# mLSTM heads kept in PSUM through square, root and gating, with the causal addition of the second tile placed first

## The chip, the core and the metric

The kernel runs on one core of a Trainium2 chip. It is written for the five engines of the core directly: TensorE (PE) multiplies, VectorE (DVE), ScalarE (ACT) and GpSimd (POOL) work element by element, and SyncE (SP) issues the loads. Each has its own queue that runs in the order written, and they wait for one another by semaphores. The metric is the device time of one execution in microseconds, the median of several runs.

## The reference

256 tokens of width 1024 pass through a stack of blocks: feed-forward layers, one mLSTM mixer, one differential attention, a second model part with convolution and attention. The change lies in the mLSTM mixer alone. With four heads, keys of 128 and values of 256 columns, in two chunks of 128 tokens, what matters is:

```
d   = where(causal, b[t] - b[s] + li[s], -inf)          # b: running sum of the log forget gates
m_t = max(b[t] + m, max over s of d)
w   = exp(d - m_t);  s_inter = exp(b + m - m_t)
qk  = (q k^T) * w
num = qk v + s_inter * (q C)
den = sum(qk) + s_inter * (q n)
h   = num / max(|den|, exp(-m_t))
h   = h * rsqrt(mean(h*h over the head) + EPS) * head_norm
return (sigmoid(o) * h) @ w_out
```

## The kernel before, in words

All large products are made in three parts, so that they keep fp32 accuracy: a rounded weight `w_hi`, the rest `w_lo`, and the same two parts of the activations (`xT_hi`, `xT_lo`). Weights come in slots of 2048 columns. For every slot SP loads `w_raw`, ACT rounds it to `w_hi` (L548, 1.9 us, called through `ahead`, four slots in advance), POOL subtracts to get `w_lo` (L519, four operations of 128x512), and PE runs twelve matmuls of 512 columns per slot and tile of 128 tokens (L1614 to L1622). The order of all other work is written out by hand for each engine.

The mLSTM stage has twelve slots of the input product ("MI", six chunks of 512 columns: q, k, two of v, two of the output gate o) and four of the output product ("MO"). PE fits the small mLSTM products between the tiles of chunks 2 to 5 (`chunk(c, amid)`):

- `spread(t)` brings the per-token gate terms of tile t into PSUM (`tb[:, 0]`); DVE's `causal_max(t)` adds the causal mask (L1183) and takes the maximum of each head (L1186). ACT turns the masked terms into exponentials (L715, L723).
- `turn_qk(0)` and `turn_qk(1)` (L1848) transpose q and k into `tb` after the first and the second tile of chunk 4; ACT copies them out (L732). Before the first of them PE waits for `m_am_ready` 2, which DVE gives when the negated maximum of tile 1 is written (L1206).
- The scores (L1855), the state (L1878) and its use (L1894), the transposed weights (L1861) and the two numerators (L1867) follow. Tile 0's numerators go to `gu`, tile 1's to `acc[:, :, 0:512]`.
- DVE multiplies the numerators with 1/denominator into `m_h` in SBUF (L1250; for tile 1 L1256 adds the parts and L1258 multiplies). ACT squares `m_h` and sums each head (L754). DVE takes the root in eleven steps on four columns (`rsqrt_steps`, L996 to L1005), each of which waits for the one before (`link`). The output gate is a sigmoid from PSUM into `m_sig` (L743, `output_gate(c, t)`), multiplied with the gain (L1265, `gate_gain(c, t)`). Last come four products per tile (L1279).
- `t_of_h(t)` lets PE transpose the result (L1667) after the third tile of chunk 5 (t = 0) and inside the output product (t = 1). It waits for `m_y_ready`.

`acc`, `gu` and `tb` are PSUM; `arena` in the rows is the large SBUF buffer that holds all `m_...` tiles. `pair(c, t)` is the PSUM half in which chunk c of tile t is accumulated: `acc[:, t, 0:512]` for c = 4, `acc[:, t, 512:1024]` for c = 5.

## Time and profile before

| what | value |
|---|---|
| median of 3 runs | 1434.67 us (1431.86 to 1436.09) |
| the profiled execution: its own time | 1433.08 us |
| its span, first to last instruction | 1431.2 us |
| PE busy | 1378.9 us (96%) |
| POOL busy | 1135.1 us (79%) |
| ACT busy | 658.3 us (46%) |
| DVE busy | 462.4 us (32%) |
| mean granted clock of PE | 0.990 |

The profile is of one execution. Busy times count each engine by itself, and they overlap. Idle time of DVE or ACT says nothing as long as PE does not wait for them. A granted clock of 1.00 is 2.4 GHz on PE, 0.50 is 1.2 GHz. The mLSTM stage lies at about 216 to 315 us of the span.

### The profile page before, as it was taken

What the parts mean: (1) busy time and instruction counts of PE and PEld (TensorE: products, weight loads), DVE (VectorE), ACT (ScalarE), POOL (GpSimd) and SP (SyncE); (2) the same over time, 40 slices, a digit from 0 to 9 for tenths busy, and PEclk for the clock granted to TensorE, in tenths of its full rate; (3) what the DMA queues carried; (4) which work ended last, traced back from release to release, by engine and by line L of the source; (5) the groups of instructions that cost most, each with busy time, mean ns of one, the idle gap of its engine ahead of it and who ended that gap; (6) DMA issues with size and microseconds to landing.
All of it is one profiled execution on the core that took longest, in us unless ns stands there. A gap on an engine that the chain in (4) does not pass through costs nothing.

```text
span 1431.2 us, 18160 instructions
## 1 busy us (share of the span) xinstructions
PE 1378.9 (96%) x6396; PEld 1127.5 (79%) x6396; DVE 462.4 (32%) x1108; ACT 658.3 (46%) x763; POOL 1135.1 (79%) x912
## 2 busy tenths in 40 slices
PE   7999999989999999999999789999999999999996
PEld 5888878877888877888888567888877877788785
DVE  6011044464000165210013665100156134552234
ACT  5444345536434365453435565443446443544431
POOL 5999977649999968899997509989877976679873
PEclk9999999999999999999999899999999999999999
DMA  8666544526665545656565406656554544346541
GB/s 258 209 205 206 192 160 174 165 74 218 191 194 178 199 151 193 192 192 195 176 196 185 136 1 191 206 186 194 177 174 165 194 160 147 120 146 234 185 141 42
DMA packets 160669, 246.95 MB, mean 173 GB/s; under 512 B 8892, under 2 KB 99812, under 8 KB 160484
## 3 DMA queue, kind: packets, MB, share of 16 engines
q1 hardware_dynamic: 158324, 239.42, 51.4%
q10 hardware_dynamic: 2288, 6.75, 1.3%
q8 instruction: 37, 0.61, 0.2%
q14 instruction: 20, 0.16, 0.0%
HBM read 245.10 MB, written 1.05 MB: 172 GB/s over the span
## 4 chain that ended last, share of the span: by engine, by line
POOL 46%; PE 35%; issue 15%; DVE 2%; ACT 1%; DMA 0%; POOLq 0%; ACTq 0%; DVEq 0%
POOL w_lo L519 46%; PE acc L1614 5%; PE acc L1617 5%; PE acc L1615 5%; PE gu L1614 3%; PE gu L1615 3%; PE gu L1617 3%; PE acc L1647 1%; PE acc L1653 1%; PE acc L1650 1%; PE gu L2004 1%; PE tb L1614 1%; PE tb L1617 1%; PE tb L1615 1%; PE tb L2013 1%
## 5 line engine op out<-in xcount | busy, mean ns | idle before, releaser
L519 POOL TENSOR_TENSOR w_lo<-w_raw,w_hi 128x512 fp32r<-128x512 f32 x896 | 1130.0, 1301 | 272.2 <-ACT w_hi L548 272.2
L548 ACT CAST w_hi<-w_raw 128x2048 fp32r<-128x2048 f32 x225 | 424.8, 1907 | 117.6 <-DMA w_raw<-in_w_ffn_in 34.1
L1614 PE MATMUL gu<-w_hi,xT_hi 128*128 128x512 f32 x832 | 331.4, 398 | 5.0 <-DVE w_lo L1545 2.8
L1615 PE MATMUL gu<-w_lo,xT_hi 128*128 128x512 f32 x832 | 325.7, 391 | 0.0
L1617 PE MATMUL gu<-w_hi,xT_lo 128*128 128x512 f32 x708 | 276.8, 391 | 0.0
L1614 PE MATMUL acc<-w_hi,xT_hi 128*128 128x512 f32 x544 | 218.7, 402 | 3.5 <-DVE xT_lo L1033 2.6
L1615 PE MATMUL acc<-w_lo,xT_hi 128*128 128x512 f32 x544 | 212.8, 391 | 0.0
L1617 PE MATMUL acc<-w_hi,xT_lo 128*128 128x512 f32 x512 | 200.8, 392 | 0.0
L1614 PEld LDWEIGHTS gu<-w_hi,xT_hi 128*128 128x128 f32 x832 | 157.3, 189 | 37.3 <-DVE xT_lo L1033 3.2
L1615 PEld LDWEIGHTS gu<-w_lo,xT_hi 128*128 128x128 f32 x832 | 157.5, 189 | 31.2 <-issue 0.2
L1092 DVE SCALAR_TENSOR_TENSOR arena<-gu,rstd,arena 128x256 f32<-128x256 f32 x88 | 42.3, 484 | 371.2 <-ACT arena L622 371.0
L1617 PEld LDWEIGHTS gu<-w_hi,xT_lo 128*128 128x128 f32 x708 | 133.4, 188 | 28.3
L622 ACT ACTIVATE arena<-gu,rstd 128x256 f32<-128x256 f32 x88 | 41.3, 474 | 201.0 <-PE gu L1617 196.1
L1614 PEld LDWEIGHTS acc<-w_hi,xT_hi 128*128 128x128 f32 x544 | 102.9, 189 | 24.6 <-issue 3.7
L1615 PEld LDWEIGHTS acc<-w_lo,xT_hi 128*128 128x128 f32 x544 | 103.0, 189 | 19.9 <-issue 0.2
L1617 PEld LDWEIGHTS acc<-w_hi,xT_lo 128*128 128x128 f32 x512 | 96.6, 189 | 20.8
L1647 PE MATMUL acc<-w_hi,hT_hi 128*128 128x512 f32 x336 | 103.9, 391 | 0.0
L1653 PE MATMUL acc<-w_hi,hT_lo 128*128 128x512 f32 x336 | 103.7, 390 | 0.0
L1650 PE MATMUL acc<-w_lo,hT_hi 128*128 128x512 f32 x336 | 103.6, 390 | 0.0
L1099 DVE TENSOR_TENSOR hT_lo<-tb,hT_hi 128x512 fp32r<-128x512 f32 x40 | 27.7, 692 | 208.1 <-ACT hT_hi L638 208.1
L638 ACT CAST hT_hi<-tb 128x512 fp32r<-128x512 f32 x40 | 23.4, 585 | 123.4 <-PE tb L1702 123.4
L1653 PEld LDWEIGHTS acc<-w_hi,hT_lo 128*128 128x128 f32 x336 | 63.1, 188 | 13.1
(300 smaller groups left out, 1289.3 us busy)
## 6 DMA issues: line engine op xcount, KB each, us to landing
w_raw<-in_w_ffn_in SPq DMA_DIRECT2D x176, 512.0 KB, 4.7
w_raw<-in_w_ffn_out SPq DMA_DIRECT2D x88, 512.0 KB, 4.2
w_raw<-in_w_in SPq DMA_DIRECT2D x80, 512.0 KB, 4.5
w_raw<-in_mlstm_w_in SPq DMA_DIRECT2D x24, 512.0 KB, 4.6
w_raw<-in_w_ple_gate SPq DMA_DIRECT2D x16, 512.0 KB, 4.3
w_raw<-in_w_kv SPq DMA_DIRECT2D x16, 512.0 KB, 4.5
w_raw<-in_mlstm_w_out SPq DMA_DIRECT2D x8, 512.0 KB, 4.5
w_raw<-in_diff_w_q SPq DMA_DIRECT2D x8, 512.0 KB, 4.1
```

What stands on the lines that cost most here:

```text
L519: ins = pool.tensor_tensor(w_lo[:, slot.spl, cols], w_raw[:, slot.raw, cols], w_hi[:, slot.spl, cols].bitcast(F32), ALU.subtract)
L548: nc.scalar.copy(w_hi[:, slot.spl, :], w_raw[:, slot.raw, :]).then_inc(hi_ready, 1)
L622: nc.scalar.activation(sg[:, t, :], gu[:, t, 0:CH], ACT.Silu, scale=rstd[:, 2 * m + t:2 * m + t + 1]).then_inc(silu_ready, 1)
L638: nc.scalar.copy(hT_hi[:], tb[:, 0, :].rearrange("p (k c) -> p k c", k=2)).then_inc(ht_hi_ready, 1)
L1092: v.scalar_tensor_tensor(hs[:, t, :], gu[:, t, CH:2 * CH], rstd[:, 2 * m + t:2 * m + t + 1], sg[:, t, :], ALU.mult, ALU.mult).then_inc(h_r ...
L1099: v.tensor_tensor(hT_lo[:], tb[:, 0, :].rearrange("p (k c) -> p k c", k=2), hT_hi[:].bitcast(F32), ALU.subtract).then_inc(ht_lo_ready, 1)
L1614: mm(out, xh, wh, start=(half == 0 and k == 0), stop=False)
L1615: mm(out, xh, wl, start=False, stop=False)
L1617: last = mm(out, xl, wh, start=False, stop=(half == 1 and k == 3))
L1647: mm(acc[:, t, 512 * half:512 * half + 512], a_hi[:, k, tok(t)], w(w_hi, half), start=st, stop=False)
L1650: mm(acc[:, t, 512 * half:512 * half + 512], a_hi[:, k, tok(t)], w(w_lo, half), start=False, stop=False)
L1653: last = mm(acc[:, t, 512 * half:512 * half + 512], a_lo[:, k, tok(t)], w(w_hi, half), start=False, stop=sp_)
```

## The change

Three edits, all in the mLSTM stage.

1. On DVE, `causal_max(1)` moves ahead of the small differences for tile 0's exponents, and its addition releases the new semaphore `m_spread_used`. PE waits for that before `turn_qk`, no longer for the finished maximum. On ACT, the rounding `ahead(s0 + 8)` and the copies of the turned q move ahead of the small exponentials.
2. The heads stay in PSUM. The product with 1/denominator is gone as an operation: ACT squares the numerators with 1/denominator as its scale, and DVE multiplies the finished root with 1/denominator (four columns). The last products read the numerators from `gu`. Tile 1's parts are added into `gu` after tile 0's products. The intermediate values of the root (`mean`, `tmp`, the last step) lie in `tb[:, 1]`.
3. The output gate's sigmoid is written in place in PSUM, and `gate_gain` reads it there; PE's second numerators wait for `m_gain_ready`. The gate of chunk 5, tile 0 moves ahead of the rounding `ahead(s0 + 11)`.

The diff, cut to its core:

```diff
@@ ScalarE, mlstm
                 ins.then_inc(m_w_ready, 1)
+                ahead(At(s0 + 8))
+                def turned_qk(i):
+                    for w in (2 * i, 2 * i + 1):
+                        act.wait_ge(m_pl_in_psum, w + 1)
...
+                turned_qk(0)
                 act.wait_ge(m_exps, 1)
                 nc.scalar.activation(m_exp0, m_exp0, ACT.Exp).then_inc(m_exped, 1)
-                ahead(At(s0 + 8))
                 act.wait_ge(m_am_ready, 2)
...
-                for w in range(4):
...
-                    if w == 1:
-                        ahead(At(s0 + 9))
+                ahead(At(s0 + 9))
+                turned_qk(1)
                 ahead(At(s0 + 10))
...
-                    nc.scalar.activation(m_sig[:, t, 512 * (c - 4):512 * (c - 4) + 512], pair(c, t),
-                                         ACT.Sigmoid, scale=rstd[:, 2 * m + t:2 * m + t + 1]
-                                         ).then_inc(m_o_gate, 1)
+                    nc.scalar.activation(pair(c, t), pair(c, t), ACT.Sigmoid,
+                                         scale=rstd[:, 2 * m + t:2 * m + t + 1]).then_inc(m_o_gate, 1)
...
-                    act.wait_ge(m_h_ready, t + 1)
+                    if t == 0:
+                        act.wait_ge(m_num_in_psum, 1)
+                        act.wait_ge(m_rden_ready, 1)
+                    else:
+                        act.wait_ge(m_h_ready, 1)
                     for h in range(MH):
                         ins = nc.scalar.activation(squares[:, MDV * h:MDV * h + MDV],
-                                                   m_h[:, t, MDV * h:MDV * h + MDV], ACT.Square,
+                                                   gu[:, h // 2, MDV * (h % 2):MDV * (h % 2) + MDV], ACT.Square,
+                                                   scale=m_rden[:, 4 * t + h:4 * t + h + 1],
                                                    accum_out=m_hssq[:, 4 * t + h:4 * t + h + 1])
...
                 head_sums(0)
+                output_gate(5, 0)
                 ahead(At(s0 + 11))
-                output_gate(5, 0)
@@ VectorE, mlstm
-                    link(v.tensor_tensor(m_am[:, t, :]...
+                    v.tensor_tensor(m_am[:, t, :]...
+                                    ).then_inc(m_spread_used, 1)
+                    dve.wait_ge(m_spread_used, t + 1)
...
                 link(v.tensor_copy(m_lrow, tb[:, 1, 24:32]))
-                link(v.tensor_tensor(m_prev, m_lrow[:, 0:4], m_lrow[:, 4:8], ALU.add))
+                causal_max(1)
                 link(v.scalar_tensor_tensor(m_exp0[:, 0:4], m_b[:, 0:4], -1.0, m_mx[:, 0:4], ALU.mult, ALU.subtract))
                 v.tensor_tensor(m_exp0[:, 4:8], m_a[:, 0:4], m_lrow[:, 4:8], ALU.subtract).then_inc(m_exps, 1)
-                causal_max(1)
+                link(v.tensor_tensor(m_prev, m_lrow[:, 0:4], m_lrow[:, 4:8], ALU.add))
                 link(v.tensor_tensor(m_mx[:, 4:8], m_mx[:, 4:8], m_prev, ALU.max))
...
-                link(v.reciprocal(m_rden, m_den))
-                dve.wait_ge(m_num_in_psum, 1)
-                v.tensor_tensor(heads(m_h[:, 0, :]), gu[:].rearrange("p a (b c) -> p (a b) c", b=2),
-                                per_head(m_rden[:, 0:4]), ALU.mult).then_inc(m_h_ready, 1)
+                v.reciprocal(m_rden, m_den).then_inc(m_rden_ready, 1)
+                dve.wait_ge(m_rden_ready, 1)
...
-                        ins = v.tensor_tensor(h1, acc[:, half, 0:512], h1, ALU.add)
-                    link(ins)
-                    v.tensor_tensor(heads(m_h[:, 1, :]), heads(m_h[:, 1, :]), per_head(m_rden[:, 4:8]), ALU.mult
-                                    ).then_inc(m_h_ready, 1)
+                        ins = v.tensor_tensor(gu[:, half, :], acc[:, half, 0:512],
+                                              m_h[:, 1, 512 * half:512 * half + 512], ALU.add)
+                    ins.then_inc(m_h_ready, 1)
...
-                    return v.tensor_tensor(m_sig[:, t, cols], m_sig[:, t, cols], gain_bc[:, cols], ALU.mult)
+                    v.tensor_tensor(m_sig[:, t, cols], pair(c, t), gain_bc[:, cols], ALU.mult
+                                    ).then_inc(m_gain_ready, 1)
...
+                h_mean, h_tmp, h_root = (tb[:, 1, 4 * i:4 * i + 4] for i in range(3))
                 for t in range(TILES):
+                    c = slice(4 * t, 4 * t + 4)
+                    if t:
+                        dve.wait_ge(t_lo_ready, 4 * T["MO"] + 2)
                     dve.wait_ge(m_hsums, t + 1)
-                    rsqrt_steps(m_hssq[:, c], m_hmean[:, c], m_hz[:, c], nt_[:, 0:4], 1.0 / MDV)
+                    rsqrt_steps(m_hssq[:, c], h_mean, m_hz[:, c], h_tmp, 1.0 / MDV, h_root)
+                    v.tensor_tensor(m_hz[:, c], h_root, m_rden[:, c], ALU.mult)
+                    gate_gain(5, t)
+                    dve.wait_ge(m_gain_ready, 2 + t + 1)
                     for h in range(MH):
-                        if h == 2:
-                            link(gate_gain(5, t))
-                        ins = v.scalar_tensor_tensor(m_h[:, t, cols], m_h[:, t, cols],
+                        ins = v.scalar_tensor_tensor(m_h[:, t, cols], gu[:, h // 2, MDV * (h % 2):MDV * (h % 2) + MDV],
...
                     if t == 0:
+                        dve.wait_ge(m_y_ready, 1)
                         second_h()
@@ TensorE, mlstm
-                    pe.wait_ge(m_am_ready, 2)
+                    pe.wait_ge(m_spread_used, 2)
...
-                    pe.wait_ge(m_o_gate, 2)
+                    pe.wait_ge(m_gain_ready, 2)
                     numerator(1, lambda h: acc[:, h // 2, MDV * (h % 2):MDV * (h % 2) + MDV])
...
-                pe.wait_ge(m_h_ready, 2)
+                pe.wait_ge(m_h_ready, 1)
```

VectorE at the maximum of tile 1, from the copy of the last row to the keys' scaling. Before:

```order
L1199 COPY arena<-tb 128x8
L1200 TENSOR_TENSOR arena<-arena 128x4
L1202 SCALAR_TENSOR_TENSOR arena<-arena 128x4
L1203 TENSOR_TENSOR arena<-arena 128x4
L1183 TENSOR_TENSOR arena<-tb,causal 128x512
L1186 TENSOR_REDUCE arena<-arena 128x4
L1205 TENSOR_TENSOR arena<-arena 128x4
L1206 TENSOR_SCALAR arena<-arena 128x4
```

The same stretch of VectorE now:

```order
L1213 COPY arena<-tb 128x8
L1195 TENSOR_TENSOR arena<-tb,causal 128x512
L1200 TENSOR_REDUCE arena<-arena 128x4
L1215 SCALAR_TENSOR_TENSOR arena<-arena 128x4
L1216 TENSOR_TENSOR arena<-arena 128x4
L1217 TENSOR_TENSOR arena<-arena 128x4
L1218 TENSOR_TENSOR arena<-arena 128x4
L1219 TENSOR_SCALAR arena<-arena 128x4
```

The addition of 128x512 and the reduction moved ahead of three operations of four columns; what the maximum needs is the same.

VectorE from the reciprocal's followers to the turned heads of tile 0 (product with 1/denominator, gain products, root, last products, tile 1's sum). Before, with the middle of the root left out at the cut:

```order
L1250 TENSOR_TENSOR arena<-gu,arena 128x1024
L1265 TENSOR_TENSOR arena<-arena 128x512 x2
L996 TENSOR_SCALAR arena<-arena 128x4
...
L1004 TENSOR_TENSOR nt_<-nt_,arena 128x4
L1005 SCALAR_TENSOR_TENSOR arena<-nt_,arena 128x4
L1279 SCALAR_TENSOR_TENSOR arena<-arena 128x256 x2
L1265 TENSOR_TENSOR arena<-arena 128x512
L1279 SCALAR_TENSOR_TENSOR arena<-arena 128x256 x2
L1256 TENSOR_TENSOR arena<-acc,arena 128x512 x2
L1258 TENSOR_TENSOR arena<-arena 128x1024
```

The end of that stretch of VectorE now:

```order
L1015 TENSOR_TENSOR tb<-tb,arena 128x4
L1017 SCALAR_TENSOR_TENSOR tb<-tb,arena 128x4
L1289 TENSOR_TENSOR arena<-tb,arena 128x4
L1276 TENSOR_TENSOR arena<-acc,arena 128x512
L1294 SCALAR_TENSOR_TENSOR arena<-gu,arena 128x256 x4
L1268 TENSOR_TENSOR gu<-acc,arena 128x512 x2
```

The first product and the last one (1024 columns each) are gone, one of four columns is new, and every operation from the root to the sum has a PSUM operand.

## Rows read from the trace of the kernel before

**Rows 1.** What PE waited for, whole run: us in total, times, longest.

```profile
PE tb L1667 <- DVE arena L1279: 4.4, 1, 4.4
PE tb L1848 <- DVE arena L1206: 1.5, 1, 1.5
```

**Rows 2.** Busy time by stretch: PE, PEld, DVE, ACT, POOL, then PE's clock, DMA.

```profile
254.00:262.00 8.00, 6.52 (x32) 5.07 (x31) 5.40 (x12) 4.91 (x10) 7.11 (x6) 1.00 0.72 231
290.00:294.00 4.00, 0.89 (x4) 0.89 (x5) 3.96 (x7) 0.00 (x0) 1.25 (x1) 0.78 0.37 91
294.00:298.00 4.00, 4.00 (x14) 3.33 (x13) 3.91 (x6) 1.83 (x6) 0.00 (x0) 0.50 0.49 171
325.00:500.00 175.00, 172.85 (x786) 142.61 (x785) 26.96 (x59) 77.02 (x71) 160.69 (x129) 1.00 0.61 196
```

**Rows 3.** PE in order of time, place 1: start us, us, what, [idle before].

```profile
256.96 0.39 PE L1617 MATMUL acc<-w_hi,xT_lo 128*128 128x512 f32 x1
258.83 1.09 PE L1848 MATMUL tb<-ident,arena 128*128 128x128 f32 x8 [1.48 <-DVE arena L1206]
...
266.13 1.06 PE L1855 MATMUL tb<-arena 128*128 128x128 f32 x8
```

**Rows 4.** VectorE in order of time, place 1.

```profile
254.61 1.20 DVE L1202 SCALAR_TENSOR_TENSOR arena<-arena 128x4 f32<-128x4 f32 x1
255.84 1.21 DVE L1203 TENSOR_TENSOR arena<-arena 128x4 f32<-128x4 f32 x1
256.98 0.68 DVE L1183 TENSOR_TENSOR arena<-tb,causal 128x512 f32<-128x512 f32 x1
...
258.41 0.16 DVE L1205 TENSOR_TENSOR arena<-arena 128x4 f32<-128x4 f32 x1
```

**Rows 5.** ScalarE in order of time, place 1.

```profile
257.20 1.88 ACT L548 CAST w_hi<-w_raw 128x2048 fp32r<-128x2048 f32 x1
258.99 1.28 ACT L723 ACTIVATE arena<-arena 128x128 f32<-128x128 f32 x4
...
260.27 1.05 ACT L732 COPY arena<-tb 128x512 f32<-128x512 f32 x2
```

**Rows 6.** GpSimd in order of time, place 1.

```profile
259.16 15.30 POOL L519 TENSOR_TENSOR w_lo<-w_raw,w_hi 128x512 fp32r<-128x512 f32 x12 [0.90 <-ACT w_hi L548]
```

**Rows 7.** PE in order of time, place 2 and one tile later.

```profile
288.29 0.39 PE L1617 MATMUL acc<-w_hi,xT_lo 128*128 128x512 f32 x1
293.11 1.97 PE L1667 MATMUL tb<-ident,arena 128*128 128x128 f32 x8 [4.43 <-DVE arena L1279]
...
299.57 0.40 PE L1614 MATMUL acc<-w_hi,xT_hi 128*128 128x512 f32 x1
...
307.76 1.04 PE L1667 MATMUL tb<-ident,arena 128*128 128x128 f32 x8
...
311.39 0.39 PE L1614 MATMUL acc<-w_hi,xT_hi 128*128 128x512 f32 x1
```

**Rows 8.** VectorE in order of time, up to place 2.

```profile
273.38 0.16 DVE L1236 TENSOR_TENSOR arena<-acc,arena 128x4 f32<-128x4 f32 x1 [3.48 <-PE acc L1890]
...
284.19 0.17 DVE L996 TENSOR_SCALAR arena<-arena 128x4 f32<-128x4 f32 x1 [0.65 <-ACT squares L754]
...
286.20 1.20 DVE L1004 TENSOR_TENSOR nt_<-nt_,arena 128x4 f32<-128x4 f32 x1
...
288.69 2.85 DVE L1279 SCALAR_TENSOR_TENSOR arena<-arena 128x256 f32<-128x256 f32 x2
...
292.17 0.88 DVE L1279 SCALAR_TENSOR_TENSOR arena<-arena 128x256 f32<-128x256 f32 x2
```

**Rows 9.** ScalarE in order of time, place 2.

```profile
281.48 0.59 ACT L749 COPY arena<-tb 128x512 f32<-128x512 f32 x1 [3.76 <-PE tb L1861]
282.37 0.42 ACT L754 ACTIVATE squares<-arena 128x256 bf16<-128x256 f32 x1 [0.30 <-DVE arena L1250]
```

**Rows 10.** Groups by line: busy us, mean ns, then the engine's idle time before.

```profile
L1092 DVE SCALAR_TENSOR_TENSOR arena<-gu,rstd,arena 128x256 f32<-128x256 f32 x88 | 42.3, 484 | 371.2 <-ACT arena L622 371.0
```

25 lines of the change are left out of this document (13 added, 12 removed).

## Prediction

> **What bounds the kernel now.** The first view is the list of what TensorE (PE) waited for. Over the whole run it is busy 1378.9 of 1431.2 us, so time can only be won where PE stands still or runs at a low clock. Two entries of that list lie in the code that changes: 4.4 us for the tile-0 heads (VectorE, L1279) and 1.5 us for the maximum of tile 1 (VectorE, L1206) [rows 1]. The second view is the table of stretches. It shows a third loss that no list of waits has: behind the 4.4 us wait the granted clock reads 0.78 and then 0.50 (1.2 instead of 2.4 GHz) while PE is busy all the time. Around the 1.5 us wait it stays at 1.00, and in 325 to 500 us PE is busy 172.85 of 175 us, so nothing there can take up a start that comes earlier [rows 2].
>
> The third view is the order of time at the two places.
>
> Place 1. PE's last matmul of the first tile of chunk 4 starts at 256.96; rows of that kind start 0.23 apart, so the turns of q could start at 257.19. They start at 258.83, which is 1.64 us lost [rows 3]. VectorE is what is late. Two operations of four columns took 1.20 and 1.21 us, since both read SBUF twice while GpSimd was working; then came the causal addition with 0.68 and the reduction, and the small operation at 258.41 took 0.16 [rows 4]. At that moment GpSimd stood still: it paused 0.90 us before 259.16 for a rounding of ScalarE [rows 6].
>
> Place 2. PE's last matmul before the turn of the heads starts at 288.29, so the turn could start at 288.52. It starts at 293.11: 4.59 us lost. The eight turns and twelve matmuls behind it take from 293.11 to 299.57, 6.46 us; the same eight and twelve, one tile later, take from 307.76 to 311.39, 3.63 us. The low clock cost 2.83 us [rows 7]. VectorE is late again: the chain of the root starts at 284.19, nine steps take 2.01 us, then GpSimd's slot begins and the next step takes 1.20 us, and the first two products take 2.85 us where the last two take 0.88 [rows 8].
>
> All three together are 1.64 + 4.59 + 2.83 = 9.06 us, the most that these places can give.
>
> **The change, part by part.** Times below are those of the old run, as if nothing before had moved.
>
> *Causal addition of tile 1 first, and q and k turned when it is done.* The addition now takes the place of the small operation of 254.61 and ends at 254.61 + 0.68 = 255.3 [rows 4], well before PE asks at 257.19. The wait goes: +1.64 us. What is late next? ScalarE now does the next rounding (1.88 us) ahead of the small exponentials, then the two copies of q [rows 5], so its queue holds nothing that PE needs earlier. But GpSimd then has its slot ready and no longer pauses [rows 6], so the small operations of VectorE behind the reduction all meet it. The reduction ends at 255.3 + 0.7 = 256.0. Until the negated maximum of tile 1 there are now four steps that wait for the one before (two exponents, the maximum, its negation). If each takes 1.25 us, as the two in [rows 4], the maximum is ready at 261.0 instead of 258.8. Behind it ScalarE needs four exponentials (1.28), the small one (0.2), a rounding (1.9) and the first copy of k (0.55) [rows 5], which gives 264.95. PE asks for k at 266.13 - 1.64 = 264.49 [rows 3], so it waits 0.45 us. Had the steps met no GpSimd (0.2 each, 256.8), there would be no wait; one GpSimd operation more (15.30 / 12 = 1.28 us [rows 6]) would make it 1.7 and take back the whole gain. I take 0.45, since the nearest rows are the two of 1.2 us: **place 1 gives 1.2 us, from 0 to 1.64**.
>
> *Heads stay in PSUM, with 1/denominator as a scale.* The old product with 1/denominator, ahead of the squares, is gone. ScalarE can start the squares when its copy of the turned weights is done, at 281.48 + 0.5 = 282.0 instead of 282.37 [rows 9]: 0.4 us. The squares themselves read 256 columns of PSUM instead of SBUF and I leave them as they are. The eleven steps of the root now start at 284.19 - 0.4 = 283.8. Each reads at most one operand from SBUF, so GpSimd does not matter to them. At the rate of [rows 8], 2.01 us for nine, with one odd gap in it, eleven take 2.2: 286.0. The product of the root with 1/denominator adds one step of 0.2: 286.2. The gain product for tile 0 (128x512, one PSUM operand) costs 0.68, as the causal addition [rows 4]: 286.9. Its gate is ready, because ScalarE now does it straight after the squares and before the rounding. Four products from PSUM have 484 ns each as in [rows 10], and two in a row take 0.88 [rows 8]: 1.7 us together, 288.6. With 0.06 to pass it on, PE turns the heads at 288.65 instead of 293.11, and waits 0.13 us.
>
> **Place 2 gives 4.59 - 0.13 = 4.45 us**. The 2.83 us of the low clock should go too, as the only long stand before it is this one, and 1.5 us at place 1 left the clock at 1.00 [rows 2].
>
> *What else is added, and what hides it.* The two gain products for columns 0 to 511 now read PSUM (0.68 each) and PE's second numerators wait for them. They run straight after the reciprocal, some 3 us before PE gets there: nothing. The sum of the two parts of tile 1 is written back to PSUM and waits for tile 0's products; two operations of 0.68 replace these two and one of 1024 columns, so it is shorter. It ends at 290.0, the scaled turns at 291.3, and PE asks for the rounded ones at 288.65 + 3.63 = 292.3 [rows 7]: about 1 us of cover. If that went, each us of delay would cost one. Tile 1 then repeats the chain: squares from about 292 to 293.7, root, gain and four products to 298.5. PE turns it 307.76 - 299.57 = 8.2 us behind its start at 292.3 [rows 7], at 300.5: 2 us of cover. GpSimd's last slot of the stage (4 x 1.3 us) moves 0.8 us later against PE, which uses it first some 8 us after it is done. The later slots, their loads on the SP queue and the gain load of ScalarE's queue all hang on PE's progress, and move with it.
>
> *A rule against it.* The four-column operation that reads PSUM takes 0.16 us [rows 8], and the causal addition with a PSUM operand is no slower than other rows of its width [rows 4]: by the rows PSUM costs nothing extra here. The Trainium skill, page "Perfetto Trace Analysis", section "Optimizing Scalar/DVE Operations", gives VectorE about 60 ns of access per instruction on SBUF and about 125 on PSUM. By that, an estimate from its figures, the seventeen operations between sums and product would take 1.1 us more and the total would be 1427.3 us.
>
> **Sum.** 1.2 + 4.45 + 2.83 = 8.5 us. The profiled execution took 1433.08 us (span 1431.2): it would be 1424.6. The median of the three runs before is 1434.67, 1.6 above it; against that the forecast is **1426.2 us**.
>
> **Rivals.**
>
> 1. *A soft miss.* Some of the seventeen chained operations of tile 0 (twelve small, one gain product, four products) are passed on late, or k comes one GpSimd operation (1.28 us) later at place 1. For it: no row of before has such a chain that writes PSUM at every step, and one handoff in the old chain, inside the 2.01 us of [rows 8], took 0.26 us more than its neighbours; five such make 1.3. Against it: the 0.16 us of [rows 8]. Either costs about 1.3 us: **1427.5**.
>
> 2. *The clock falls all the same.* PE has a short wait at each place and the clock still drops once for as long as before. For it: the clock fell about 4 us into the old wait and VectorE is just in time at best. Against it: 1.00 around the wait of 1.5 us [rows 2]. With 1 us of wait on top the gain is 8.5 - 2.83 - 1 = 4.7: **1430.0**.
>
> 3. *The gain is there but does not arrive.* A wait of PE further on (a slot of GpSimd, a load) takes the early start up. For it: GpSimd is busy 160.69 of 175 us in 325 to 500. Against it: PE is busy 172.85 in the same stretch [rows 2]. It would give **1433** or so, no measurable difference.
>
> 4. *Slower.* The mechanism is the handoff through PSUM in tile 0's and tile 1's chain. If every one of the seventeen operations costs 0.26 us more, the 4.4 us of place 2 are eaten up; from there on it is slower. At 0.5 us each, tile 0 comes 8.5 us later than forecast and PE waits 8.6 instead of 4.6; tile 1's products end at 288.65 + 8.5 + 9.85 + 8.5 = 315.5 against PE's demand at 288.52 + 8.6 + 6.46 + 8.2 = 311.8, another 3.7. With place 1's 1.2 us the net is 6.5 us more: **1441**. Only the one gap of 0.26 us speaks for it.
>
> 5. *It does not do what it says*: the causal addition comes first but PE still waits for the maximum through k. That is place 1 at zero, and is inside 1.
>
> **How the numbers follow.** Forecast 0.62, rival 1 0.14, rival 2 0.10, rival 3 0.10, rival 4 0.04. The measurement of this kernel can tell about 0.3%, 4.3 us, from no change, which puts the line at 1430.4. Forecast, rival 1 and most of rival 2 lie below it: faster 0.83. Rival 3 and the rest of 2: same 0.13. Slower 0.04. The range starts at the full 9.06 us with place 1 unhampered and 3 us for the spread that the runs before show (1431.86 to 1436.09): 1422.5. It ends where rival 2 does, with a little of the spread: 1431.0. What is left out is rival 3, rival 4 and a bit of the rest.
>
> **What would show it.** Right: no wait of PE for q's turn; the causal addition of tile 1 near 255; PE's wait before the turn of the heads under 0.5 us; a clock of 1.00 from 254 to 326; small PSUM steps at 0.2 us apart while GpSimd works; PE's start of the next FFN 8 to 9 us earlier. Wrong: steps of the root that start 0.3 us apart or more; small operations of about 1.2 us in the root; a wait of PE for k over 1 us; a clock below 1.00 near 290; an earlier start of the FFN that is gone by 500 us.

## The result, and the profile after

| | before | after |
|---|---|---|
| median | 1433.54 us, 4 runs (1431.86 to 1436.09) | 1425.62 us, 4 runs (1425.27 to 1427.89) |
| ratio, 95% interval | | 0.9946 (0.9933 to 0.9959) |
| the profiled execution, its span | 1433.08, 1431.2 | 1427.89, 1426.0 |
| mean granted clock of PE in the profile | 0.990 | 0.990 |

The change saves 7.8 us (5.9 to 9.6). Forecast were 8.5. The changed kernel was run a second time in the experiments and gave 1426.57 us (6 runs) against 1434.35 (19 runs), ratio 0.9945 (0.9933 to 0.9957).

First the list of PE's waits, changed kernel, 245 to 345 us of the span (us in total, times, longest). It answers [rows 1].

```profile
PE tb L1683 <- DVE x_res L1080: 1.6, 2, 0.8
PE tb L1871 <- ACT arena L727: 1.4, 1, 1.4
PE gu L1630 <- ACT xT_hi L580: 0.7, 1, 0.7
```

Both waits of [rows 1] are gone. The 4.4 us have no successor; the 1.5 us have one of nearly the same size, for the turned k, which ACT copies at L727. The first and the third row belong to a boundary of the feed-forward part behind the stage, and the old kernel has them too (1.5 and 0.7 us).

The table of stretches of the changed kernel (us, busy PE, PEld, DVE, ACT, POOL, then PE's clock) answers [rows 2]:

```profile
286.00:290.00 4.00, 4.00 (x22) 3.17 (x22) 3.93 (x9) 0.34 (x1) 4.00 (x4) 1.00 0.00 0
290.00:294.00 4.00, 4.00 (x19) 3.29 (x19) 2.53 (x10) 3.33 (x11) 1.03 (x1) 1.00 0.39 109
294.00:298.00 4.00, 4.00 (x19) 3.31 (x18) 3.23 (x11) 0.00 (x0) 0.00 (x0) 1.00 0.46 158
325.00:500.00 175.00, 175.00 (x794) 144.66 (x794) 23.01 (x52) 77.69 (x71) 159.76 (x128) 1.00 0.62 195
```

PE is busy throughout, and at full clock where it had 0.78 and 0.50. Third, PE in order of time, both places (start us, us, what, [idle before]). It answers [rows 3, 7].

```profile
256.32 1.04 PE L1864 MATMUL tb<-ident,arena 128*128 128x128 f32 x8
...
265.15 1.05 PE L1871 MATMUL tb<-arena 128*128 128x128 f32 x7 [1.44 <-ACT arena L727]
...
287.40 0.39 PE L1633 MATMUL acc<-w_hi,xT_lo 128*128 128x512 f32 x1
287.76 1.09 PE L1683 MATMUL tb<-ident,arena 128*128 128x128 f32 x8
...
299.60 1.03 PE L1683 MATMUL tb<-ident,arena 128*128 128x128 f32 x8
```

These five rows, set against their counterparts, give the whole account. In both kernels take how much earlier the row starts, and then what each step adds to it. The changed kernel came into the stage 0.9 us early (its rounding there starts at 206.08 instead of 206.99), before any changed line, which is luck of that run.

| row | before | after | earlier by | added |
|---|---|---|---|---|
| rounding ahead of the stage | 206.99 | 206.08 | 0.91 | |
| turn of q | 258.83 | 256.32 | 2.51 | 1.60 |
| k and the scores (L1855, L1871) | 266.13 | 265.15 | 0.98 | -1.53 |
| last matmul before the turn of the heads | 288.29 | 287.40 | 0.89 | -0.09 |
| turn of the heads, tile 0 | 293.11 | 287.76 | 5.35 | 4.46 |
| turn of the heads, tile 1 | 307.76 | 299.60 | 8.16 | 2.81 |

Place 1 gave 1.60 us and took 1.53 back ten microseconds later. Place 2 gave 4.46, and the clock 2.81. The stage is 7.2 us shorter in this profile.

The later run takes something away again: the roundings of ScalarE start 8.1 us early up to the differential attention (near 790 us) and 5.1 us early after it. Between 800 and 850 us the clock was low for 20.5 us in the profile of after (three stretches from 806.8) and for 13.7 in that of before (two, from 814.5). Which of these stretches cost time is taken up near the end. So the one profiled execution is only 5.2 us faster than the one of before while the medians are 7.9 apart. The other three timed runs of after took 1425.3 to 1425.8 us.

### The profile page after: what moved, and what is told of

It reads as the page before. It is cut to its first block, busy times and chain, and to the rows that moved or that the text cites. A ratio compares the mean times of both kernels' runs of the same rounds, so it can differ in the third digit from the quotient of the medians.

```text
span 1426.0 us, 18163 instructions
## 1 busy us (share of the span) xinstructions
PE 1379.2 (97%) x6396; PEld 1126.7 (79%) x6396; DVE 460.1 (32%) x1108; ACT 659.1 (46%) x763; POOL 1133.7 (80%) x912
## 4 chain that ended last, share of the span: by engine, by line
POOL 46%; PE 34%; issue 16%; DVE 2%; ACT 1%; DMA 1%; POOLq 0%; SPq 0%; ACTq 0%; DVEq 0%
POOL w_lo L522 46%; PE acc L1630 5%; PE acc L1633 5%; PE acc L1631 5%; PE gu L1630 3%; PE gu L1631 3%; PE gu L1633 3%; PE acc L1663 1%; PE acc L1669 1%; PE acc L1666 1%; PE gu L2020 1%; PE tb L1630 1%; DMA w_raw<-in_w_ffn_in 1%; PE tb L1633 1%; PE tb L1631 1%
## 5 line engine op out<-in xcount | busy, mean ns | idle before, releaser
L1666 PEld LDWEIGHTS acc<-w_lo,hT_hi 128*128 128x128 f32 x336 | 63.1, 188 | 13.1
```

The costliest lines, as they stand in the source:

```text
L1666: mm(acc[:, t, 512 * half:512 * half + 512], a_hi[:, k, tok(t)], w(w_lo, half), start=False, stop=False)
```

## Place 1: where the 1.6 us went

VectorE of the changed kernel in order of time, the answer to [rows 4]:

```profile
253.84 0.69 DVE L1195 TENSOR_TENSOR arena<-tb,causal 128x512 f32<-128x512 f32 x1 [0.33 <-PE tb L1848]
...
255.28 0.89 DVE L1215 SCALAR_TENSOR_TENSOR arena<-arena 128x4 f32<-128x4 f32 x1
256.21 1.20 DVE L1216 TENSOR_TENSOR arena<-arena 128x4 f32<-128x4 f32 x1
257.33 1.33 DVE L1217 TENSOR_TENSOR arena<-arena 128x4 f32<-128x4 f32 x1
258.70 1.21 DVE L1218 TENSOR_TENSOR arena<-arena 128x4 f32<-128x4 f32 x1
259.94 1.20 DVE L1219 TENSOR_SCALAR arena<-arena 128x4 f32<-128x4 f32 x1
```

ScalarE, which answers [rows 5], and GpSimd, which answers [rows 6]:

```profile
261.18 1.28 ACT L735 ACTIVATE arena<-arena 128x128 f32<-128x128 f32 x4 [3.04 <-DVE arena L1219]
262.73 1.88 ACT L551 CAST w_hi<-w_raw 128x2048 fp32r<-128x2048 f32 x1
264.52 1.06 ACT L727 COPY arena<-tb 128x512 f32<-128x512 f32 x2
```

```profile
236.42 25.95 POOL L522 TENSOR_TENSOR w_lo<-w_raw,w_hi 128x512 fp32r<-128x512 f32 x20 [3.75 <-ACT w_hi L551]
```

GpSimd runs without a pause from 236 to 262, as forecast, and VectorE moves at its pace: taken one by one, GpSimd's operations start at 256.12, 257.35, 258.60, 259.85 and 261.08, and the five small operations of VectorE end 0.05 to 0.06 us after these. But five of them stand between the reduction and the negated maximum, not four. The one left out of the count is L1217, which does not wait for the operation ahead of it. So the maximum is there at 261.1 on this run's clock. On the forecast's it would be 261.1 + 0.9 = 262.0 against 261.0. Behind it ScalarE has the exponentials and a rounding of 1.9 us, and only then the copy of k. PE waits 1.44 us for that.

### Edit 1 undone

The order of VectorE and ScalarE at place 1, and PE's wait, are those of before:

```diff
                 link(v.tensor_copy(m_lrow, tb[:, 1, 24:32]))
-                causal_max(1)
+                link(v.tensor_tensor(m_prev, m_lrow[:, 0:4], m_lrow[:, 4:8], ALU.add))
                 link(v.scalar_tensor_tensor(m_exp0[:, 0:4], ...
                 v.tensor_tensor(m_exp0[:, 4:8], ...
-                link(v.tensor_tensor(m_prev, m_lrow[:, 0:4], m_lrow[:, 4:8], ALU.add))
+                causal_max(1)
...
-                    pe.wait_ge(m_spread_used, 2)
+                    pe.wait_ge(m_am_ready, 2)
```

> The changed kernel with the first edit undone: old order of VectorE and ScalarE around the maximum of tile 1, and PE waits for the maximum before it turns q. In the trace of the changed kernel PE no longer waits for q, but waits 1.4 us for the first copy of k (ScalarE), because seven small VectorE operations in a row take 0.9 to 1.3 us each while GpSimd works. Theory: the first edit gives nothing, so the mLSTM stage is as long as in the changed kernel to within 0.2 us, with a wait of 1.5 us for q in place of the one of 1.4 us for k. Rival (the forecast): the edit was worth 1.2 us, and this kernel is 1.2 us slower in the stage.

1428.07 us (4 runs) against 1433.87 (11), ratio 0.9955 (0.9940 to 0.9969). PE's only wait between 245 and 315 us:

```profile
PE tb L1862 <- DVE arena L1217: 1.5, 1, 1.5
```

In the trace the stage is as much shorter as in the changed kernel: 7.2 us. By these two profiles the whole gain is edits 2 and 3; edit 1 exchanges a wait of 1.5 us for q for one of 1.4 for k (another profile further down has it otherwise). The median is 2.4 us above the changed kernel's, or 1.3 by the ratios. With intervals of 2 us on each side that is no certain difference, so that edit 1 is worth nothing is shown by the length of the stage in the traces and not by the medians. The expectation counts one too many: six small operations of VectorE were slow in the changed kernel, and the seventh took 0.16 us.

### Maximum first, small exponents behind

```diff
                 causal_max(1)
-                link(v.scalar_tensor_tensor(m_exp0[:, 0:4], ...
-                v.tensor_tensor(m_exp0[:, 4:8], ...
                 link(v.tensor_tensor(m_prev, m_lrow[:, 0:4], m_lrow[:, 4:8], ALU.add))
                 link(v.tensor_tensor(m_mx[:, 4:8], m_mx[:, 4:8], m_prev, ALU.max))
                 v.tensor_scalar(m_negmx[:, 4:8], m_mx[:, 4:8], -1.0, None, ALU.mult).then_inc(m_am_ready, 1)
+                link(v.scalar_tensor_tensor(m_exp0[:, 0:4], ...
+                v.tensor_tensor(m_exp0[:, 4:8], ...
```

ScalarE's small exponential for tile 0 moves too, from ahead of the maximum's exponentials to behind the next rounding (not shown here).

> The changed kernel, with tile 1's maximum and its negation directly behind the reduction, the exponents of tile 0 behind them, and ScalarE's small exponentials moved behind the next rounding. Theory (the chain of small operations that meets GpSimd holds back the maximum): the negated maximum comes two to three GpSimd operations (2.5 to 3.7 us) earlier, k is copied in time, PE's wait for k goes and the stage is 1.4 us shorter than in the changed kernel. Rival (ScalarE's own queue, rounding and copies, sets k's time): the wait stays within 0.3 us of 1.4.

1426.09 us (4 runs), ratio 0.9948 (0.9933 to 0.9962); the stage is 7.8 us shorter than before, 0.65 better than the changed kernel. The wait for k is gone and another stands in its place:

```profile
PE gu L1894 <- DVE arena L1223: 0.8, 1, 0.8
```

VectorE now has seven slow small operations where the changed kernel has six, and behind them its last one, the keys' scaling, is late:

```profile
264.14 1.84 DVE L1223 TENSOR_TENSOR arena<-arena 128x512 f32<-128x512 f32 x1
```

The maximum sets k, the exponents set the scaled keys, and PE needs both within a few microseconds. This order takes 0.65 us out and moves the rest of the lateness elsewhere.

### k copied before the rounding

```diff
-                ahead(At(s0 + 9))
                 turned_qk(1)
+                ahead(At(s0 + 9))
                 ahead(At(s0 + 10))
```

> The changed kernel, with the copies of k ahead of ScalarE's rounding instead of behind it. Theory: k is late by a sum (seven slow small operations, four exponentials, one rounding), so taking the rounding of 1.9 us out is enough too: the wait of 1.4 us goes, and the stage is 1.4 us shorter. Rival (the chain alone is too late, k would still be waited for): some wait of 0.5 us or more stays. If the later rounding holds GpSimd and so a slot up, PE would show a new wait for w_lo.

1426.34 us (4 runs), ratio 0.9950 (0.9933 to 0.9967). PE has no wait at all between 245 and 315 us. ScalarE:

```profile
263.76 1.05 ACT L727 COPY arena<-tb 128x512 f32<-128x512 f32 x2
264.70 3.71 ACT L551 CAST w_hi<-w_raw 128x2048 fp32r<-128x2048 f32 x2
```

The negated maximum is as late as before, but the copies no longer stand behind 1.9 us of rounding. The stage is 8.9 us shorter than before, close to the 9.06 that the prediction named as the most to be had. The median does not show it, and its profiled run lost 3.2 us in the differential attention, where the clock was low for 20.5 us as in the profile of after.

### The small operations read PSUM

The differences read the gate terms from `tb`, and the maxima of tile 1 are written to `gu` before its products need it. The exponents of tile 0 also move ahead of the causal addition, so only two small operations are left between the reduction and the negated maximum (added lines, cut):

```diff
+                v.scalar_tensor_tensor(m_exp0[:, 0:4], tb[:, 1, 16:20], -1.0, m_mx[:, 0:4], ALU.mult, ALU.subtract)
+                v.tensor_tensor(m_exp0[:, 4:8], m_a[:, 0:4], tb[:, 1, 28:32], ALU.subtract).then_inc(m_exps, 1)
+                link(v.tensor_tensor(m_prev, tb[:, 1, 24:28], m_lrow[:, 4:8], ALU.add))
+                mx_own, mx_all = gu[:, 0, 0:4], gu[:, 0, 4:8]
+                causal_max(1, mx_own)
+                link(v.tensor_tensor(mx_all, mx_own, m_prev, ALU.max))
```

> The changed kernel, with one operand of each small operation around tile 1's maximum in PSUM (the maximum in a free corner of gu, the last row and tile 0's sums read where the matmul left them) and the exponents of tile 0 ahead of the addition. Theory (a small operation is slow only when both its inputs are in SBUF while GpSimd works): each takes 0.16 to 0.2 us instead of 0.9 to 1.3, the negated maximum is ready near 256 instead of 261, no wait for k, stage 1.4 us shorter than the changed kernel, and 1.4 + 7.9 = about 9.3 us faster than before (ratio 0.9935). Rival (small operations are slow from their chained waits, whatever they read): they stay near 1.2 us each, nothing is won.

1425.65 us (6 runs, 1423.46 to 1430.12), ratio 0.9945 (0.9931 to 0.9959). VectorE, while GpSimd runs without a pause from 236.08 to 267.46:

```profile
254.97 0.17 DVE L1220 TENSOR_TENSOR gu<-gu,arena 128x4 f32<-128x4 f32 x1
255.18 0.16 DVE L1221 TENSOR_SCALAR arena<-gu 128x4 f32<-128x4 f32 x1
```

The maximum is ready at 255.3 instead of 261.1, and no wait is left at either place. The same operations, beside the same GpSimd work, are fast once an operand lies in PSUM: it is the place of the operands that made them slow. That the wait for k went is not the doing of PSUM alone, since the new order took three operations off the path as well.

Two inputs in SBUF are not the only case. L1219 in the rows of the changed kernel, the negation, is a TENSOR_SCALAR with a single tensor input, from SBUF to SBUF, and took 1.20 us like its neighbours; reading `gu` (L1221 above) it takes 0.16. The Trainium skill states the rule in "SBUF — State Buffer", section "🔬 SBUF: two separate sides": a VectorE operation in a mode that uses two ports, or one with two SBUF inputs against a GpSimd operation that reads SBUF, takes a port pair that the two engines share, in turns, each for its whole length. The trace agrees, 0.84 to 1.33 us for either kind against 0.16. Not every input from SBUF is slow, though: the reduction of 512 columns (L1200, one input) took 0.69 us beside a working GpSimd, as it does elsewhere.

The stage was 9.0 us shorter up to 336 us. Then the clock fell for 3.4 us at the next boundary of the feed-forward part and took 1.3 of that back:

```profile
322.00:326.00 4.00, 3.85 (x11) 3.12 (x12) 3.29 (x12) 3.30 (x7) 4.00 (x5) 0.63 0.67 198
```

## Place 2: which part of the edit did it

The answer to [rows 8], VectorE up to the turn of tile 0's heads:

```profile
283.04 0.17 DVE L1007 TENSOR_SCALAR tb<-arena 128x4 f32<-128x4 f32 x1 [3.70 <-ACT squares L764]
...
285.25 0.16 DVE L1289 TENSOR_TENSOR arena<-tb,arena 128x4 f32<-128x4 f32 x1
285.33 0.68 DVE L1276 TENSOR_TENSOR arena<-acc,arena 128x512 f32<-128x512 f32 x1
286.04 1.66 DVE L1294 SCALAR_TENSOR_TENSOR arena<-gu,arena 128x256 f32<-128x256 f32 x4
```

The answer to [rows 9], ScalarE, and GpSimd's slot:

```profile
281.07 0.48 ACT L764 ACTIVATE squares<-gu,arena 128x256 bf16<-128x256 f32 x1
...
283.43 0.66 ACT L749 ACTIVATE acc<-acc,rstd 128x512 f32<-128x512 f32 x1 [0.42 <-PE acc L1633]
```

```profile
285.99 5.04 POOL L522 TENSOR_TENSOR w_lo<-w_raw,w_hi 128x512 fp32r<-128x512 f32 x4 [11.39 <-ACT w_hi L551]
```

Twelve small steps 0.20 apart, the gain product and four products of 1.66 us together; these four run beside GpSimd and are not slowed. But GpSimd begins only at 285.99, when the small steps are over. In [rows 8] it began two steps before their end. So two things could have saved the root: the intermediate values in PSUM, or the gate that now goes ahead of the rounding, so that GpSimd gets its slot later. Three kernels tell these apart. Each is the changed kernel with one or both of:

```diff
-                    rsqrt_steps(m_hssq[:, c], h_mean, m_hz[:, c], h_tmp, 1.0 / MDV, h_root)
-                    v.tensor_tensor(m_hz[:, c], h_root, m_rden[:, c], ALU.mult)
+                    rsqrt_steps(m_hssq[:, c], m_hmean[:, c], m_hz[:, c], nt_[:, 0:4], 1.0 / MDV)
+                    v.tensor_tensor(m_hz[:, c], m_hz[:, c], m_rden[:, c], ALU.mult)
```

```diff
                 head_sums(0)
-                output_gate(5, 0)
                 ahead(At(s0 + 11))
+                output_gate(5, 0)
```

The root in SBUF alone:

> The changed kernel with the root's intermediate values back in SBUF (mean, product and result), all else as changed. In the trace of the changed kernel the twelve small steps of tile 0 end at 285.4, 0.6 us before GpSimd's slot starts at 286.0. Theory (the root is fast because ScalarE rounds the slot later, behind the gate, not because its values lie in PSUM): nothing changes, the steps stay 0.2 us apart and the turn of the heads is not late by more than 0.1 us. Rival (PSUM operands are what keeps GpSimd off the root): steps of 1.2 us appear and the heads are 1 us late or more.

1427.38 us (3 runs), ratio 0.9949 (0.9929 to 0.9970). The last small step, and GpSimd:

```profile
284.96 0.16 DVE L1289 TENSOR_TENSOR arena<-arena 128x4 f32<-128x4 f32 x1
```

```profile
285.72 5.04 POOL L522 TENSOR_TENSOR w_lo<-w_raw,w_hi 128x512 fp32r<-128x512 f32 x4 [11.39 <-ACT w_hi L551]
```

No step is slow and PE does not wait for the heads. The rounding first alone:

> The changed kernel with the old order of ScalarE at tile 0: the rounding of the stage's last slot first, then the gate of chunk 5. GpSimd's slot then starts near 285.0, within the last steps of the root, and the gate is ready near 285.5. Theory: with the root's values in PSUM these steps stay at 0.2 us; only the gate is later by 0.2 to 0.3 us, so PE waits about 0.3 us for the heads. Rival (position of GpSimd's slot decides, whatever the operands): the last steps take 1.2 us and PE waits 1.5 us or more.

1427.1 us (3 runs), ratio 0.9946 (0.9923 to 0.9968). GpSimd starts at 283.82, ahead of the last two steps of the root, and these still take 0.16 and 0.17 us; PE waits 0.2 us for the heads. Both together:

> Both at once: the root in SBUF and the rounding ahead of the gate. Theory: now GpSimd's slot meets steps with two SBUF inputs, the last one to three of them take 1.2 us each, and PE waits 1 to 2.5 us for the heads; the PSUM operands and the order of ScalarE are two ways to the same thing, and only without both the loss comes back. Rival (neither matters, the gain of place 2 comes from the products out of PSUM and the missing first product): PE waits under 0.5 us.

1429.76 us (6 runs), ratio 0.9972 (0.9959 to 0.9985). The last small step has both inputs in SBUF and meets GpSimd, which started at 285.27:

```profile
285.47 1.14 DVE L1289 TENSOR_TENSOR arena<-arena 128x4 f32<-128x4 f32 x1
```

```profile
PE tb L1683 <- DVE arena L1294: 0.9, 1, 0.9
```

So either half is enough for the root by itself, and only without both is it held up by GpSimd again; one step is caught, which costs 0.9 us of wait. In the medians only this last kernel is apart, by some 3 to 4 us; how much of that is more than the 0.9 us of its stage is open (one profile each).

With that the 4.46 us of place 2 can be put down to rows. The start of the root, with the 0.91 us of the run taken off, is 0.25 us earlier. From the root's start to the first product it was 288.69 - 284.19 = 4.50 us and is 285.33 - 283.04 = 2.29: 2.2 us, for the most part two caught steps of 1.2. From there to the last product, with the gain product in it, it was 2.85 + 0.68 + 0.88 and is 0.68 + 1.66: 2.0 us, two caught products of 1.4 that now read PSUM beside a busy GpSimd.

## The clock behind the wait

### The wait of before, filled

Useless matmuls (sixteen products of activations and weights, written to `tb` and then overwritten) stand where PE waited for the heads in the kernel before:

```diff
                 def t_of_h(t):
+                    if t == 0:
+                        for n in range(16):
+                            mm(tb[:, 0, :], xT_hi[:, n % 8, tok(0)], w_hi[:, At(s0 + 11).spl, 0:512],
+                               start=True, stop=True)
```

> The kernel before, with sixteen matmuls of 512 columns into a free PSUM bank, whose result nothing reads, in PE's queue ahead of the wait for tile 0's heads. They take 3.6 us of the 4.6 us that PE stands still there. Theory (the low clock behind the wait comes from PE's idleness): the clock stays at 1.00 from 254 to 326, the turn of the heads still starts when VectorE is done, and the stage is 2.8 us shorter than before (2.6 to 3.0). Rival (the fall has its own time, whatever PE does, or the fillers delay the turn): the clock falls all the same and the stage is as long as before or up to 0.5 us longer.

1434.06 us (10 runs) against 1434.1 (19), ratio 1.0004 (0.9993 to 1.0015): no difference. The stretches of its profile:

```profile
290.00:294.00 4.00, 3.13 (x19) 2.44 (x18) 3.93 (x7) 0.00 (x0) 0.84 (x1) 1.00 0.44 127
294.00:298.00 4.00, 4.00 (x19) 3.04 (x18) 3.59 (x5) 2.25 (x8) 0.00 (x0) 1.00 0.38 135
...
330.00:334.00 4.00, 4.00 (x14) 3.16 (x13) 3.03 (x12) 3.56 (x7) 4.00 (x4) 0.66 0.89 266
1400.00:1410.00 10.00, 7.10 (x32) 5.56 (x32) 9.20 (x5) 1.17 (x2) 5.59 (x5) 0.90 0.00 0
```

The clock behind the wait is 1.00, where [rows 2] has 0.78 and 0.50, and the stage is 2.5 us shorter up to 336 us, near the 2.8 expected. So the wait is what made it fall. Then it fell for 3.4 us from 329.3, which took 1.6 back, and near 1405 PE waited 2.9 us for VectorE where the profile of before has 1.6 of wait for GpSimd, and the clock fell there too. One profile shows that the gain at the heads was there and went in other places. Whether it went there in the other nine runs, and why, stays open.

### The heads later, in two steps

The changed kernel with three, and with six, useless multiplications on VectorE before tile 0's products:

```diff
                     dve.wait_ge(m_gain_ready, 2 + t + 1)
+                    if t == 0:
+                        for n in range(3):
+                            link(v.tensor_tensor(m_ksc, pair(5, 0), gain_bc[:, 0:512], ALU.mult))
```

Three:

> The changed kernel with three useless 128x512 multiplications on VectorE (0.69 us each, into the keys' scaled copy, which is not read any more) ahead of tile 0's products with the gate, so that the heads come 2.1 us later. Theory (a wait costs its length until the clock falls, and the fall costs 2.8 on top): TensorE waits 2.0 to 2.2 us for the heads. Waits of 2.8 in the attention stood before falls and waits of 0.7 to 1.4 mostly did not, so 2.1 is expected to hold the clock: 2.1 us slower than the changed kernel. Rival (the fall's cost goes with the wait's length, from the first microsecond): 2.1 + 1.4 = 3.5 us slower.

1429.74 us (6 runs), ratio 0.9970 (0.9958 to 0.9981), 3.2 us more than the changed kernel beside it.

```profile
PE tb L1686 <- DVE arena L1297: 2.2, 1, 2.2
```

```profile
290.00:294.00 4.00, 3.99 (x16) 3.29 (x17) 3.77 (x6) 2.07 (x7) 1.05 (x1) 0.67 0.39 106
```

The wait is 2.2 us, the clock falls at 291.3 for 3.4 us, and the stage loses 3.8 us: 2.2 of wait and 1.6 of clock. My own expectation (the clock holds) was wrong and the rival's 3.5 near. Its mechanism, a cost that grows with the wait from the first microsecond, is not shown by this: waits of 1.4 to 1.5 us for q or k left the clock at 1.00 in every profile. Six:

> As the run with three multiplications, with six: the heads come 4.1 us later, close to the wait of 4.43 of the kernel before. Theory: TensorE waits 4.0 to 4.2 us, the clock falls behind it for about 6.8 us and the time is 4.1 + 2.8 = 6.9 us longer than the changed kernel's, about what was gained. Rival (the low clock at 292 in the kernel before did not come from this wait): 4.1 us longer with the clock at 1.00. Half of either difference would mean that TensorE does not set the end in this stretch.

1434.5 us (10 runs), ratio 1.0000 (0.9991 to 1.001), 7.9 us more than the changed kernel.

```profile
PE tb L1686 <- DVE arena L1297: 4.3, 1, 4.3
```

```profile
290.00:294.00 4.00, 1.80 (x9) 1.80 (x10) 3.93 (x8) 0.00 (x0) 1.06 (x1) 0.60 0.40 112
294.00:298.00 4.00, 4.00 (x12) 3.14 (x12) 2.52 (x7) 3.01 (x10) 0.00 (x0) 0.54 0.45 155
```

4.3 us of wait, 6.8 us of low clock, and a stage that is 6.9 us longer up to 336 us (4.3 and 2.6 for the clock): what the forecast said, and about the time of the kernel before. The clock fell once more at 331.8 in this profile, which makes it 8.5. The gain of place 2 can be switched off by lateness of VectorE alone, and a wait of VectorE at this place costs some 1.6 to 1.7 times its length.

## The changed kernel again, and a candidate

The changed kernel again:

> The changed kernel itself a second time, unchanged, for what one profiled execution can't tell: whether the 1.4 us wait for the turned k (turn of k at 265.15 in the first profile of it) is in every execution. Theory (phase): in the run with only the gate's rounding moved, the same vector steps at place 1 had two unlinked steps at 0.15 us where the first profile of the changed kernel had them at 1.33, with the chain 0.3 us later against GpSimd's operations, and no wait for k followed; so the profile shows a stage (the rounding before it to the one after it) of either about 7.2 us gained, with a wait for k of 1.4 and the negated maximum done near 261.2, or about 8.5 with no wait for k and the maximum done near 260.1. Rival (fixed): 1.4 us of wait again, within 0.3. The median should be within 1 us of 1425.6 either way.

1426.57 us (6 runs, 1425.38 to 1428.39). PE waits 1.5 us for k again, L1217 took 1.32 us again, and the stage is 7.2 us shorter again. So this kernel showed the wait twice, as the rival says. It is still not fixed. Seven profiles here have the very instructions of the changed kernel at place 1 (this kernel twice, root in SBUF, rounding first, both, heads 2 and 4 us later), and six of them have the wait, 1.4 or 1.5 us long. The seventh is the kernel with only the rounding moved at place 2, where they ran so on VectorE:

```profile
257.56 0.15 DVE L1217 TENSOR_TENSOR arena<-arena 128x4 f32<-128x4 f32 x1
...
260.06 0.15 DVE L1220 SCALAR_TENSOR_TENSOR arena<-arena 128x4 f32<-128x4 f32 x1
```

The maximum was a microsecond earlier, PE did not wait for k, and the stage was 8.5 us shorter up to 336 us. That later edit is not the reason, since the kernel with it and the root in SBUF has the wait. An operation that needn't wait for the one ahead slips in before GpSimd's next operation, or just misses it. The expectation's "0.3 us later" was read from the clock of the span, but GpSimd's operations came 0.2 us later too. Against them the two cases are a few hundredths of a microsecond apart: L1217 starts at 257.56 and GpSimd's next operation at 257.57 where it slips in, at 257.33 and 257.35 in the changed kernel, at 257.06 and 257.09 with the root in SBUF. What decides between them stays open. My forecast's four slow steps are what happened in that one profile, and there edit 1 was worth 1.3 us, near the 1.2 forecast; in the first two profiles of the changed kernel it was worth nothing.

The other kernel is a candidate. The small operations read PSUM, and seven useless matmuls (identity by causal mask, into columns that nothing reads) fill the waits of 0.65 and 2.81 us ahead of the low clock in the differential attention:

```diff
                         ins.then_inc(d_scores, 1)
+                    if h in (1, 2):
+                        for n in range((0, 1, 6)[h]):
+                            mm(acc[:, 1, 512:896], ident[:], causal[:], start=True, stop=True)
```

> A candidate that goes on from the small operations in PSUM: it adds useless matmuls (seven products of the identity with the causal mask, 128x384, into columns of the accumulator that nothing reads) where TensorE waits 0.65 and 2.81 us in the differential attention, before its clock falls at 806. Theory (the clock there falls behind these waits): no low clock from 806 to 817, the step of the attention from the 128th to the 160th rounding 3 to 5 us shorter than in the profile of the small operations in PSUM, median 1421 to 1423. Rival (VectorE sets that stretch, whose steps don't follow TensorE's clock): the clock holds and the time stays at 1425 to 1426. Third: the clock falls all the same, some us later, as it did when the wait for the heads was filled in the kernel before: no gain.

1425.45 us (6 runs), ratio 0.9942 (0.9929 to 0.9956). The stretch without and with the fill:

```profile
807.00:812.00 5.00, 4.26 (x20) 3.18 (x20) 4.54 (x26) 2.69 (x13) 0.00 (x0) 0.50 0.41 144
```

```profile
807.00:812.00 5.00, 4.49 (x27) 2.78 (x25) 4.61 (x25) 2.69 (x12) 0.00 (x0) 1.00 0.52 170
```

The clock is held, and the time is the same. VectorE is busy 4.54 and 4.61 of the 5 us, which fits that it sets this stretch; the equal time is what is shown. What differs between profiles and costs time lies later. Between 834 and 844 us the clock was

```profile
834.00:844.00 10.00, 9.19 (x30) 7.40 (x31) 5.34 (x17) 0.58 (x1) 0.00 (x0) 0.66 0.00 0
```

in the changed kernel, which lost 3.1 us from before the attention to after it, and 1.00 with the root in SBUF, which lost nothing. The other profiles fall in line. With every profile shifted to the changed kernel's time, the two without a low clock from 833.5 to 845 us lost nothing across the attention against the profile of before (root in SBUF, heads 2 us later). The eight with 3.4 us of it lost 1.2 to 2.0 us, and the three with 6.8 us lost 2.6 to 3.0. The longer stretch near 807 made no such difference. So a profile's loss there goes with this one fall of the clock; why it comes in some and not in others is open.

All kernels, with the part of the profile that the change touches apart from the rest. "To 336" is how much earlier than before the rounding starts that stands at 336.42 in before, less the same for the one ahead of the stage at 206.99; "to 373" is that 36 us on, behind the feed-forward boundary:

| kernel | median us | to 336 | to 373 |
|---|---|---|---|
| changed | 1425.62, again 1426.57 | 7.2, 7.2 | 7.2, 7.2 |
| edit 1 undone | 1428.07 | 7.2 | 7.2 |
| maximum first | 1426.09 | 7.8 | 7.8 |
| k before the rounding | 1426.34 | 8.9 | 8.9 |
| small operations in PSUM | 1425.65 | 9.0 | 7.6 |
| the same, attention filled | 1425.45 | 9.0 | 7.4 |
| root in SBUF | 1427.38 | 7.3 | 7.3 |
| rounding first | 1427.1 | 8.5 | 7.1 |
| root in SBUF, rounding first | 1429.76 | 6.3 | 6.3 |
| before, wait filled | 1434.06 | 2.5 | 0.9 |
| heads 2 us later | 1429.74 | 3.4 | 3.4 |
| heads 4 us later | 1434.5 | 0.2 | -1.4 |

No kernel beats the changed one by its median with any certainty, though three are 1.7 to 1.8 us better in the stage up to 336 us. Only the one with k before the rounding keeps that to 373 us. In five of the profiles (both with the small operations in PSUM, rounding first, the filled one and the last) the clock fell for 3.4 us at the feed-forward boundary near 325 and took 1.3 to 1.6 us. Three of these five have no wait for k. PE waits there three times for 0.7 us in every kernel. Why it falls in some is open.

## Why the prediction was right

The forecast of 1426.2 us came out at 1425.62. Two of its three terms held, in size and in mechanism. The third was wrong, and that the time agrees to 0.6 us is luck.

- **Place 1, 1.2 us forecast, 0.1 measured.** The turn of q gained its 1.6 us as worked out, and 1.5 of it were lost again to k. The step that failed is the count of the slow operations: "four steps that wait for the one before". There are five operations up to the negated maximum, and the fifth, L1217, was slow too although it waits for nothing. Rival 1 had named this ("k comes one GpSimd operation later") and its price, and rival 5's result, place 1 at zero, is what happened; 0.14 was too little, as six of seven profiles with these instructions show it.
- **Place 2, 4.45 us forecast, 4.46 measured.** Root steps 0.20 apart, gain product 0.68, products 1.66 (forecast 1.7), a loss of 0.13 us at PE (287.76 against 287.40 + 0.23), as forecast. One piece was mis-sized: the squares from PSUM with a scale take 0.48 us, not the 0.42 that I left them at, four of them 0.45 apart instead of 0.41. The root starts 0.25 us earlier, not 0.4. That was made good by small differences behind it. One reason was not put to the test: the root was to be fast because of its operands in PSUM, but in the changed kernel GpSimd starts only 0.6 us after the root's end, since the gate goes ahead of the rounding. The three kernels above show that either is enough.
- **The clock, 2.83 us forecast, 2.81 measured**, and confirmed from both sides: the filled wait took the fall away and the delayed heads brought it back.
- **PSUM costs nothing extra for small operations.** They have 0.16 to 0.17 us with and without PSUM operands. The estimate of 1.1 us more with the Trainium skill's figures (page "Perfetto Trace Analysis", section "Optimizing Scalar/DVE Operations") is not borne out; the measurement decides. Rival 4 had no basis beyond the one gap of 0.26 us, which did not come again.
- **Tile 1's cover held**: last products from 295.78, its turn by PE at 299.60, no wait.
- **Rival 3 was not seen in the stage's own stretch**: 8.1 us of earlier start reach 790 us unchanged. The stretch from 325 to 500, where PE is busy 175.00 of 175 us, passes it on. In the attention 3.1 us of it went in this profile, and 0 to 3 in the others, so a part of what rival 3 says did happen there.
- **From trace to median.** In the trace the stage gives 7.2 us, 1.3 less than the sum; the medians are 7.9 apart (7.8 by the ratio), and what the other 0.7 are is not known. The forecast started from the median of three runs of before, 1434.67, which came down to 1433.54 with a fourth. The sum was 1.3 us too large and the start 1.1 too high, and these two errors cancel. The profiled execution, for which the same sum says 1424.6, took 1427.89.

## What to carry to other kernels

Where small operations of VectorE run beside a busy GpSimd, count every one of them on the path, also those that wait for nothing, and ask of each whether all its operands lie in SBUF. One input is enough to be held up, as the negation shows. Giving one operand a place in PSUM frees it, at no price for operations of four columns. When a late operation is moved forward, follow the queue behind it up to the next point where another engine asks: here the time won for q was lost to k, and it would have taken a second move (the copies of k ahead of a rounding) to keep it. Price a wait of TensorE with the low clock behind it: 2.2 us cost 3.8, 4.3 us cost 6.9, and the 1.4 to 1.5 us ones cost their length.

## What was unexpected of the hardware

- A wait of 2.2 us was followed by 3.4 us of low clock, one of 4.3 by 6.8; I had expected the first to be free of it.
- With the clock held at 1.00 in place of 0.50 from 806 to 817 us no time was won, while VectorE was busy over 4.5 of 5 us.
- The same instructions have a 0.15 or a 1.33 us long operation at the same place, with starts against GpSimd's that differ by a few hundredths of a microsecond.
- A small operation with one input, from SBUF to SBUF, takes 1.20 us beside a busy GpSimd, as those with two inputs do.
- ScalarE squares 256 columns in 0.48 us from PSUM with a scale per partition and in 0.40 to 0.42 from SBUF without one; which of the two differences it is was not tried.
